# Two attention heads share one turned tile in a fused attention and mLSTM block

## The reference, cut to what matters

```
h = rms_norm(x, pre_norm_g)
aq, ak, av, az, mq, mk, mv, mo, mz, mi, mf = split_columns(h @ w_in)
ya = moba_attention(partial_rope(aq), partial_rope(ak), av)   # softmax(q k^T / 8) v, causal, 8 heads
ya = rms_norm(ya, attn_out_g) * silu(az)
ym = sigmoid(mo) * norm(mlstm(...)) * mlstm_out_g * silu(mz)
y  = concat(ya, ym) @ w_out
out = x + rms_norm(y, post_norm_g)
```

## Time and profile before

| | us |
|---|---|
| median of 3 runs | 319.71 |
| lowest, highest | 317.78, 320.05 |
| profiled execution, its own time | 318.38 |
| its span | 316.6 |
| TensorE busy | 308.4 |
| VectorE busy | 225.9 |
| ScalarE busy | 164.9 |
| GpSimd busy | 96.7 |

### The profile page before, as it was taken

How to read it: one execution, slowest core, us unless ns; L and a number is a source line. 1 busy time by engine, 2 the same in 40 slices (tenths; PEclk the granted TensorE clock), 3 DMA queues, 4 the chain that set the end, 5 groups by cost and what they waited for, 6 DMA issues and landing times.

```text
span 316.6 us, 4991 instructions
## 1 busy us (share of the span) xinstructions
PE 308.4 (97%) x1595; PEld 255.7 (81%) x1595; DVE 225.9 (71%) x509; ACT 164.9 (52%) x337; POOL 96.7 (31%) x121
## 2 busy tenths in 40 slices
PE   7999999999999999999999999999999999999992
PEld 4888888878888888888888888778888888888882
DVE  3544999748998699968998568965577766856534
ACT  3448856287345324573147573385556976453201
POOL 3701006066450114002220026592711984000000
PEclk9999999999999999999999999999999999999998
DMA  7941553956725486654865433211220474310111
GB/s 233 313 99 36 158 144 94 164 154 155 142 69 135 135 151 204 182 144 114 181 193 183 114 77 88 71 66 34 67 68 0 127 185 157 134 68 0 66 68 67
DMA packets 29177, 38.30 MB, mean 121 GB/s; under 512 B 3672, under 2 KB 15296, under 8 KB 29152
## 3 DMA queue, kind: packets, MB, share of 16 engines
q1 hardware_dynamic: 27424, 34.51, 36.7%
q0 software_dynamic: 1568, 3.34, 7.3%
q10 hardware_dynamic: 160, 0.14, 0.1%
HBM read 33.68 MB, written 4.29 MB: 120 GB/s over the span
## 4 chain that ended last, share of the span: by engine, by line
PE 82%; DVE 7%; issue 4%; DMA 3%; ACT 2%; DVEq 0%; POOLq 0%; POOL 0%; SPq 0%; ACTq 0%
PE bank L1501 21%; PE bank L1503 21%; PE bank L1502 20%; PE bank L1553 4%; PE bank L1849 3%; PE bank L1793 3%; DMA w_raw<-in_w_in 3%; PE bank L1814 3%; PE bank L1646 2%; DVE w_lo L1061 2%; DVE farena L1173 1%; PE bank L1743 1%; PE bank L1534 1%; PE bank L1804 1%; PE bank L1647 1%
## 5 line engine op out<-in xcount | busy, mean ns | idle before, releaser
L788 ACT ACTIVATE w_hi<-w_raw 128x512 fp32r<-128x512 f32 x71 | 43.7, 626 | 63.1 <-PE bank L1503 50.8
L1501 PE MATMUL bank<-w_hi,xT_hi 128*128 128x512 f32 (+1 forms) x180 | 72.5, 403 | 0.0
L1503 PE MATMUL bank<-w_hi,xT_lo 128*128 128x512 f32 (+1 forms) x180 | 69.7, 387 | 0.0
L1502 PE MATMUL bank<-w_lo,xT_hi 128*128 128x512 f32 (+1 forms) x180 | 69.4, 385 | 0.0
L1061 DVE TENSOR_TENSOR w_lo<-w_raw,w_hi 128x512 fp32r<-128x512 f32 x64 | 45.6, 724 | 10.3 <-ACT w_hi L788 10.2
L1501 PE MATMUL bank<-xT_hi,w_hi 128*128 128x512 f32 x128 | 50.8, 397 | 0.0
L1503 PE MATMUL bank<-xT_hi,w_lo 128*128 128x512 f32 x128 | 50.1, 392 | 0.0
L1502 PE MATMUL bank<-xT_lo,w_hi 128*128 128x512 f32 x128 | 50.0, 390 | 0.0
L1503 PEld LDWEIGHTS bank<-w_hi,xT_lo 128*128 128x128 f32 x180 | 33.8, 188 | 7.1
L1501 PEld LDWEIGHTS bank<-w_hi,xT_hi 128*128 128x128 f32 x180 | 33.9, 188 | 5.9 <-issue 0.4
L1502 PEld LDWEIGHTS bank<-w_lo,xT_hi 128*128 128x128 f32 x180 | 34.0, 189 | 5.5
(11 more groups left out here) (215 smaller groups left out, 583.4 us busy)
## 6 DMA issues: line engine op xcount, KB each, us to landing
w_raw<-in_w_in SPq DMA_DIRECT2D x72, 256.0 KB, 3.0
w_raw<-in_w_out SPq DMA_DIRECT2D x16, 256.0 KB, 2.9
kq_rows<-stage SPq DMA_DIRECT2D x8, 256.0 KB
gy<-kq_rows SPq DMA_DIRECT2D x8, 256.0 KB, 3.5
gy<-in_x SPq DMA_DIRECT2D x4, 512.0 KB, 5.9
out_y<-gy SPq DMA_DIRECT2D x7, 256.0 KB, 2.0
farena<-in_x SPq DMA_DIRECT2D x4, 256.0 KB, 4.3
farena<-in_x SPq DMA_DIRECT2D x2, 512.0 KB, 6.3
```

The costliest lines, as they stand in the source:

```text
L788: a.activation(hi, raw, ACT.Copy).then_inc(w_hi_done, 1)
L1501: pe.matmul(o, hi, m_hi, start=start, stop=False)
L1502: pe.matmul(o, hi, m_lo, start=False, stop=False)
L1503: return pe.matmul(o, lo, m_hi, start=False, stop=stop)
```

## The change

Before, the two heads of a pair became two tiles of 128 rows (64 of the high part, 64 of the low part of the values), each turned by its own transpose. Now the halves are brought together ahead of the turn. In bank 2 the even head's result proper lies in rows 0 to 63 and its partner rows in 64 to 127; for the odd head the change takes rows 64 to 127 as home and 0 to 63 as partner rows. ScalarE copies the partner rows of each head (64x256) to the home rows of a tile `y2_far` (128x256) in SBUF. VectorE adds the bank's home rows to them, two instructions of 64x256, and then adds the two column halves by a reduce of `y2_far` into one tile of 128x128, the even head above, the odd one below. One transpose turns it, a step later than before (at odd steps); all eight heads of a tile fit into bank 3, and one instruction on VectorE reads the bank and divides (`ya_wide`). The next pair's products wait for the two adds. Tile 3 works as before.

The order moves too: on ScalarE the copies stand first in an odd step, on VectorE adds and reduce stand ahead of the step's mask, where the old reduce stood behind it. Division, square, norm and gate of tiles 0 to 2 come one step later, the turn of tile 2 at step 34, and four products of the output projection at step 34 and not 35. GpSimd's two normalisations are gone.

```diff
-F_SM, F_P, F_YA, F_Y = 0, 1024, 2048, 3072
+F_SM, F_P, F_YA, F_Y, F_Y2 = 0, 1024, 2048, 3072, 5120
...
-LAG_T, LAG_PV, LAG_FOLD, LAG_YT = 2, 3, 5, 6
+LAG_T, LAG_PV, LAG_FOLD, LAG_YT = 2, 3, 5, 7
...
-    (19, "ya", 0), (27, "ya", 1), (33, "ya", 2), (37, "ya", 3)])
+    (19, "ya", 0), (27, "ya", 1), (34, "ya", 2), (37, "ya", 3)])
...
-             (2, 0, [32, 32, 33, 33, 34, 34, 35, 35], 36), (2, 1, [35] * 4 + [36] * 4, 37),
+             (2, 0, [32, 32, 33, 33, 35, 35, 35, 35], 36), (2, 1, [34, 34, 34, 34] + [36] * 4, 37),
...
-    _event(_s - 3 + _late, "ya_half", _i)
-    _event(_s + 2 * _late, "ya", _i)
-    _event(_s + 3 * _late, "ya_sq", _i)
-    _event(_s + 1 + 3 * _late, "ya_ms", _i)
-    _event(_s + 1 + 4 * _late, "ya_gate", _i)
+    _event(_s + 3 * _late, "ya", _i)
+    _event(_s + 4 * _late, "ya_sq", _i)
+    _event(_s + 1 + 4 * _late, "ya_ms", _i)
+    _event(_s + 1 + 5 * _late, "ya_gate", _i)
...
-        y2 = num[:, :, 0:P]
+        y2_far = num[:].rearrange("p t c -> p (t c)")[:, 0:2 * P]
...
+        y2 = f_part(F_Y2, 2, P)
...
+            def y2_move(u):
+
+                a.wait_ge(pv_ps, u + 2)
+                if u:
+                    a.wait_ge(y2_summed, u // 2)
+                for q in range(2):
+                    to, of = slice(q * DH, (q + 1) * DH), slice((1 - q) * DH, (2 - q) * DH)
+                    a.activation(y2_far[to, :], bank[2][of, 2 * P * q:2 * P * (q + 1)], ACT.Copy).then_inc(y2_moved, 1)
+
             for s in range(STEPS):
                 events = EVENTS.get(s, ())
+                if 0 <= s - LAG_FOLD < N_WIDE and s % 2 == 1:
+                    y2_move(s - LAG_FOLD)
...
             def y2_sum(u):
 
-                v.wait_ge(pv_ps, u + 2)
-                if u:
-                    v.wait_ge(yt_ps, u)
-                v.tensor_reduce(y2, bank[2][:].rearrange("p (u a q) -> p u q a", u=2, a=2), mybir.AxisListType.X,
-                                ALU.add).then_inc(y2_done, 2)
+                n = u // 2
+                v.wait_ge(y2_moved, u + 2)
+                for q in range(2):
+                    at = slice(q * DH, (q + 1) * DH)
+                    v.tensor_tensor(y2_far[at, :], bank[2][at, 2 * P * q:2 * P * (q + 1)], y2_far[at, :],
+                                    ALU.add).then_inc(y2_read, 1)
+                v.wait_ge(y2_read, u + 2)
+                if n >= 2:
+                    v.wait_ge(yt_ps, n - 1)
+                v.tensor_reduce(y2[:, n % 2, :], y2_far.rearrange("p (a q) -> p q a", a=2), mybir.AxisListType.X,
+                                ALU.add).then_inc(y2_summed, 1)
...
+            def ya_wide(i):
+
+                rec = rrec[:, AH * i:AH * i + AH]
+                v.reciprocal(rec, rsum[:, AH * i:AH * i + AH]).then_inc(rrec_done, 1)
+                v.wait_ge(yt_ps, AH // 2 * (i + 1))
+                v.wait_ge(rrec_done, i + 1)
+                ya_free(i)
+                v.tensor_tensor(ya[:, i % 2, :].rearrange("p (h d) -> p h d", h=AH),
+                                bank[3][:].rearrange("p (h d) -> p h d", h=AH),
+                                rec.unsqueeze(2).to_broadcast([P, AH, DH]), ALU.mult).then_inc(ya_done, 1)
...
             for s in range(STEPS):
                 events = EVENTS.get(s, ())
+                if 0 <= s - LAG_FOLD < N_WIDE and s % 2 == 1:
+                    y2_sum(s - LAG_FOLD)
                 if s < NU:
                     mask(s)
-                if 0 <= s - LAG_FOLD < N_WIDE and s % 2 == 1:
-                    y2_sum(s - LAG_FOLD)
...
             def turn_y2(u):
 
-                h = u % AH
-                pe.wait_ge(y2_done, u + 1)
-                if h % 4 == 0 and u:
-                    pe.wait_ge(ya_summed, u // 4)
-                pe.transpose(bank[3][:, h % 4 * P:(h % 4 + 1) * P], y2[:, u % 2, :], ident[:]).then_inc(yt_ps, 1)
+                n = u // 2
+                pe.wait_ge(y2_summed, n + 1)
+                if n and u % AH == 0:
+                    pe.wait_ge(ya_done, u // AH)
+                pe.transpose(bank[3][:, n % 4 * P:(n % 4 + 1) * P], y2[:, n % 2, :], ident[:]).then_inc(yt_ps, 1)
 
             def wide_values(u):
 
@@ -1809,7 +1823,7 @@
                 if u == 0:
                     pe.wait_ge(mz_gated, NT)
                 elif u % 2 == 0:
-                    pe.wait_ge(y2_done, u)
+                    pe.wait_ge(y2_read, u)
...
-                if 0 <= s - LAG_YT < N_WIDE and s % 2 == 0:
+                if 0 <= s - LAG_YT < N_WIDE and s % 2 == 1:
                     turn_y2(s - LAG_YT)
-                    turn_y2(s - LAG_YT + 1)
```

More of the change, by code:

```diff
@@ L125 @@
 EVENTS = {}
-PRIORITY = ("mz", "mz_late", "z", "slot", "z_part", "part", "part_q", "ya_half", "ya", "ya_sq", "ya_ms",
+PRIORITY = ("mz", "mz_late", "z", "slot", "z_part", "part", "part_q", "ya", "ya_sq", "ya_ms",
             "ya_gate", "y_sq", "y", "y_q_sq", "y_q", "y_fin", "y_end", "cut", "turn")
@@ L471, in build @@
         pv_ps = sem("pv_ps")
-        y2_done = sem("y2_done")
+        y2_read = sem("y2_read")
+        y2_moved = sem("y2_moved")
+        y2_summed = sem("y2_summed")
         yt_ps = sem("yt_ps")
@@ L737, in _ @@
                         cut(i)
-                    elif kind == "ya" and i < NT - 2:
-                        ya_norm(i)
                     elif kind == "ya_ms":
@@ L1478, in _ @@
                 for kind, what in events:
-                    if kind == "ya_half":
-                        ya_half(*what, 0)
+                    if kind == "ya" and what[0] < NT - 1:
+                        ya_wide(*what)
                     elif kind == "ya":
-                        ya_whole(*what)
+                        ya_last()
                     elif kind == "ya_ms":
```

46 lines of the change are left out of this document (17 added, 29 removed).

## The result

The changed kernel takes **332.94 us** (median, 330.75 to 333.67), the kernel before 319.35 (317.78 to 320.05) on the same chip: a ratio of **1.044**, 95% interval 1.0405 to 1.0474. The forecast was 326.3 with a range of 321.5 to 330. The direction was right and the loss twice as large: 13.6 us where +6.6 was said. The profiled execution took 330.75 (span 329.0), against 318.38 (span 316.6).

The account below looks back on a forecast made before the run. It took TensorE's queue, busy without idle time in the attention part, as the bound. -1.3 + 4.6 + 3.3 = +6.6 us took the profiled 318.38 to 325.0; the median, 1.3 above, gave 326.3, range 321.5 to 330.

Parts of the forecast that it names:

- Transposes: TensorE's queue in the attention part: 12 of 24 transposes go, 0.11 each, saving 1.3 us.
- Bare chain: Odd steps 7 to 27: the longer series of copies, adds, reduce and mask stalls TensorE, together +4.6 us.
- A rule against the change: VectorE instruction starting in another 32-partition group waits for earlier ones; second add 0.09 later per fold, 1.0 us, outside the sum.
- Lateness: Steps 15, 17, 19, 23: ScalarE's backlog delays the copies by 1.2, 0.6, 0.2, 1.3: +3.3 us, bounds 0 and 5.
- Tail and GpSimd at no cost: Work moved to step 34 and GpSimd's two removed normalisations: neither changes TensorE's waits, cost nothing.
- Rival 3: Every stall costs a restart of about 0.2, 8 times, and ScalarE's backlog is at its upper bound: +9.9, 329.6; chance 0.15.

Follow-up runs that it names:

- same_rows: The changed kernel with both copies and both adds of a fold on the same rows, second half of the result left out: ratio 1.0273.
- light_scalar: The changed kernel with ScalarE's output-weight copies cut to an eighth of their columns and its squares to 64 of 512: ratio 1.0288.
- square_later: The changed kernel with the square, mean and gating of the attention rows of the first two tiles one step later: ratio 1.044.
- stalled_23: The kernel before with the mask behind the fold and, at step 23 alone, three more reduces of the bank ahead of the real one: ratio 1.0116.
- fed: The changed kernel with 14 idle matmuls in TensorE's queue just ahead of the values' products of step 23: ratio 1.0413.

## Why the prediction was right in kind and half in size

At step 28 the profiled execution had lost 13.3 us:

- **Transposes, -1.3: right.** 12 instructions fewer, about -1.2 of them up to step 28.
- **Bare chain, +4.6: the step that failed.** Its links, their order and the room against them were right. But it priced pairs by the start-to-start time of neighbours that work on the same rows. Light on ScalarE's backlog, steps 5 to 13 show the chain alone: 3.39 lost where the step gives 1.51 of stalls, less 0.44 for the four transposes saved by then, 1.07. Of the 2.32 missing, 1.80 are starts held up by a change of rows, as same_rows shows: 0.23 at step 5, where the prediction saw room enough and put 0, and 0.39 at each of the four folds behind it. The other 0.52 (0.13 at each of these four) I put down to the handoffs, 0.11 and 0.24 in place of 0.05; that is read from rows and was not tested. For 11 folds, at 0.36 and 0.13, and with step 5: +4.0, +1.4 and +0.2, so the term is 10.2, not 4.6.
- **"A rule against the change": weighed wrongly.** It was priced at 0.09 a fold by the second add only and left out. By what was measured it moves the second add from 0.35 to 0.45 behind the first and the mask from 0.35 to 0.46 behind the reduce, and ScalarE behaves likewise.
- **Lateness, +3.3: right in size.** 2.6 by light_scalar up to step 24, with step 15 at 1.15 (forecast 1.2), and about 1.0 more at step 23, read from rows. The cause was in part another: it was laid to the moved square, while square_later shows that the amount of work makes it, and at step 23 the division on VectorE has a part in it.
- **The clock: missing.** The fall costs 1.6 where TensorE has no other waits (stalled_23), and less in the changed kernel. There steps 24 to 28 lost 2.47 with it, and 1.50 in light_scalar without: about 1.0. While TensorE ran slowly the others caught up: its wait at step 25, 0.56 in light_scalar, is gone.
- **Tail and GpSimd at no cost: right** for the tail, 0.0 behind step 28. GpSimd's part was not measured by itself.

-1.2 + 4.6 + 4.0 + 1.4 + 0.2 + 2.6 + 1.0 + 1.0 = 13.6, against 13.3 measured. The handoffs (1.4), the lateness left at step 23 and the clock's 1.0 are read from rows or from the difference of two profiled executions, so that the close agreement is in part luck. Rival 3 had the right kind, "more than the sum", with other causes: restarts of 0.2 do not show (the stalled weight load is followed by its matmul after 0.03, 226.69 and 226.72), nor did the backlog reach its upper bound. The order deserves a word of its own, since the prediction had it in its chain but gave it no price: the mask behind the fold is 3.6 us of the total, but only with the long chain ahead of it.

## What to carry to other kernels

Before splitting one instruction into two on different rows, price the pair in full lengths, not in start-to-start times, and look which later instruction changes rows back (here the mask). A longer release chain does no harm while it fits in what the other engine has to do meanwhile; measure that room in the trace at its tightest step, and keep what others wait for (here the mask) ahead of it in the queue. Work that leaves the critical engine must find room on the others where they are fullest: here steps 14 to 27 had little, and a gain of 1.3 us did not survive in any form tried.

## What the runs showed of the hardware

- ScalarE, too, starts an instruction on other rows than its neighbour only when that has ended: 0.40 instead of 0.29 for 64x256 copies.
- VectorE's add of two SBUF operands, 64x128, went from 0.61 to 2.17 a pair while GpSimd worked in SBUF; a gating of 128x512 took 0.75 to 1.66. With one operand in PSUM the pair took 0.60 there. Where the gating started first, it kept its 0.75 and GpSimd's cut took 1.83 instead of 1.29.
- Two waits of TensorE of 1.87 and 0.65 at one step were followed by a stretch at the 1.2 GHz level (0.50 of the granted clock) that cost 1.6 us; by their mean clocks four of eight executions of that kernel had one such stretch and three had none. Waits of 0.73 and 1.23 in fed were followed by one too, waits of 1.56 and 1.10 in same_rows were not.
